# Sample units of an mLSTM decoder step: values, gates and keys turned in 32 by 32 squares by VectorE instead of by identity products on TensorE

## Chip, cores, metric

The kernel runs on one core of a Trainium2 chip. The metric is the device time of one execution in microseconds, and the time of a kernel is the median of several runs.

## What is computed

One inference step of a one-layer hybrid decoder: RMSNorm, one input projection (1024 to about 8200 columns), three parallel groups that read it, one output projection, residual and a final RMSNorm. A prompt of 2048 tokens and a sample group of 8 sequences with 8 tokens each go through the same layer. The change touches only the mLSTM group (4 heads of width 256) and of that only the sample group:

```
S    = (q k^T) * exp(Dm - m_t)                      # causal, per head
num  = w_inter * (q C) + S v
den  = w_inter * (q n) + sum(S)
h    = num / max(|den|, exp(-m_t))
C_new = w_C * C + sum_s w_s k_s v_s^T ;  n_new = w_C * n + sum_s w_s k_s
y_ml = rms_norm(sigmoid(o_pre) * h, g_head) * silu(z_ml)
```

C is a 256 by 256 matrix for each head and sequence, so the sample group has 32 of them, which are read and written.

## The kernel before

The program has three stages, one after the other on all engines: `project` (normalisation, all products with the input weights, which go to DRAM as channels by tokens), `attend` (cross-attention and convolution with their part of the output product) and `recur` (the mLSTM recurrence, its part of the output product, final norm). The change is in `recur`, the last 425 us or so.

`recur` goes over NT = 16 tiles t of 128 prompt tokens. TensorE does in each tile: `numerators(t)` (L2208, L2209), the eight state updates `update(t, j)` (L2223) with the output products of the tile before in between (`out_part(t - 1, g)`, L2256 to L2258), `scores(t + 1)` (L2184) and `turn_y(t)` (L2288, identity products that turn y). VectorE has for each tile: `add`, `first_half(t)`, `update(t, j)` with `turn_v`, `turn_keys` and `final_norm` between the updates, `second_half(t)` (L2660, L2665, which finishes y), `turn_o(t + 1)` (L2620), `score_weights(t + 1)` (L2558), `y_gate` and `y_low`. TensorE's `numerators(t + 1)` waits for `score_weights(t + 1)`.

The sample group is cut into UNITS = 8 units (4 sequences and one head each), with 32 tokens of a unit. Unit u is begun in tile t = 2u (`front_of`) and finished in tile 2u + 1 (`back_of`). Engines run their own instruction lists and meet by semaphores; the order in each list is the order of the code.

Values, output gates and keys of a unit lie in DRAM as channels by tokens, and the recurrence wants values, gates and one copy of the keys as tokens by channels, with token t of sequence j on partition 32j + t. Before the change `load_unit` on SyncE's queue fetches them as channels on 128 partitions in pieces of 8 tokens (32 bytes): four DMAs for values and gates (L1994) and two for keys (L1997). TensorE then turns them by products with the identity: four in `unit_turn_vo` (L2279) after `update(t, 6)` of an even tile, and two in `unit_front` (L2306) after `scores(t + 1)`. ScalarE takes values and gates out of PSUM in `unit_vo_back` (L2442, L2443) and the keys in its `unit_front` (L2471), scaled. The keys are also used as they are loaded, for the unit's scores (L2308), and that stays.

`load_unit` of unit u + 2 stands in SyncE's list at the end of iteration 2u + 2, behind the gates of the next tile; units 0 and 1 are loaded ahead of the loop. SyncE's list begins like this:

```python
sp.wait_ge(S["s_padded"], 3)
values(1)
load_unit(sp, 0, rest=False)
load_unit(sp, 0, states=False)
out_gates(1)
...
load_unit(sp, 1)
out_gates(2)
```

`values`, `out_gates` and `key_squares` already load the prompt tiles in squares of 32 by 32, which VectorE turns with its 32 by 32 block transposition (L2601, L2610, L2620). The prompt's keys, values and gates have been stored in that form since `project`.

## Time and profile before

| | us |
|---|---|
| median of 3 runs | 2056.63 |
| lowest and highest run | 2053.71, 2058.09 |
| the profiled execution, first to last instruction | 2055.3 |
| TensorE matmul busy in it | 2033.4 (99%) |
| VectorE busy | 1429.1 (70%) |
| ScalarE busy | 922.2 (45%) |
| GpSimd busy | 878.9 (43%) |

For the profiled execution the profile gives the span alone and no further time around it. Busy time on TensorE counts matmuls whose ends are modelled and overlap, so the distance from the start of one product to the start of the next says what a product costs, and not its duration. "L2279" is a line of the kernel before. SPq is SyncE's queue of DMA issues: the duration of its rows is the time of the issue, not of the transfer.

### The profile page before, as it was taken

How to read it: one execution, taken by the hardware profiler on the slowest of the kernel's cores; microseconds unless marked ns; L12 is line 12 of the kernel's file. 1: busy time of each engine (PE TensorE's matmuls, PEld its weight loads, DVE VectorE, ACT ScalarE, POOL GpSimd, SP SyncE). 2: the span in 40 equal slices, each digit the busy share in tenths (PEclk: the TensorE clock that was granted, in tenths of full speed). 3: DMA queues.
4: the chain of work that ended last, by engine and by line, in shares of the span. 5: the costliest groups of instructions: out<-in, count | busy, mean ns of one | idle time of the engine just before them, and what ended most of it. 6: DMA issues, size and time to landing. Idle time of an engine off the chain costs nothing.

```text
span 2055.3 us, 34212 instructions
## 1 busy us (share of the span) xinstructions
PE 2033.4 (99%) x12287; PEld 1892.5 (92%) x12287; DVE 1429.1 (70%) x2211; ACT 922.2 (45%) x1884; POOL 878.9 (43%) x720
## 2 busy tenths in 40 slices
PE   8999999999999999999999999999999999999998
PEld 5999999999999999999999999988888888888886
DVE  7667676688777666797777767644445477777774
ACT  5544445545445455454454455432224333343331
POOL 2465556575655555575555555510000122222320
PEclk9999999999999999999999999999999999999999
DMA  6634555555534555555345565677646788777754
GB/s 221 148 111 124 141 142 140 142 132 126 136 114 137 146 152 128 135 143 128 109 127 149 132 140 135 154 195 174 169 113 181 214 239 272 236 237 232 238 175 108
DMA packets 550983, 327.72 MB, mean 159 GB/s; under 512 B 283424, under 2 KB 514720, under 8 KB 550816
## 3 DMA queue, kind: packets, MB, share of 16 engines
q1 hardware_dynamic: 512672, 306.66, 55.1%
q10 hardware_dynamic: 36992, 14.68, 2.9%
q0 software_dynamic: 1152, 4.19, 0.6%
q8 instruction: 99, 1.62, 0.3%
q14 instruction: 68, 0.56, 0.1%
HBM read 232.16 MB, written 93.31 MB: 158 GB/s over the span
## 4 chain that ended last, share of the span: by engine, by line
PE 95%; DVE 2%; issue 1%; ACT 1%; ACTq 1%; DMA 0%; SPq 0%; DVEq 0%; POOLq 0%; POOL 0%
PE bank L707 21%; PE bank L709 21%; PE bank L708 21%; PE bank L2256 3%; PE bank L2258 3%; PE bank L2257 3%; PE bank L2223 3%; PE bank L2208 3%; PE bank L1653 1%; PE bank L1605 1%; PE bank L1655 1%; PE bank L1654 1%; PE bank L1640 1%; PE bank L1642 1%; PE bank L1641 1%; PE bank L2184 1%
## 5 line engine op out<-in xcount | busy, mean ns | idle before, releaser
L707 PE MATMUL bank<-xh,wh 128*128 128x352 f32 x2688 | 869.4, 323 | 2.1 <-DVE stage L1110 0.9
L709 PE MATMUL bank<-xh,wl 128*128 128x352 f32 x2688 | 865.9, 322 | 0.0
L708 PE MATMUL bank<-xl,wh 128*128 128x352 f32 x2688 | 862.9, 321 | 0.0
L1092 DVE TENSOR_TENSOR wl<-raw,wh 128x512 fp32r<-128x512 f32 x384 | 423.1, 1104 | 204.0 <-ACT wh L855 202.8
L707 PEld LDWEIGHTS bank<-xh,wh 128*128 128x128 f32 x2688 | 504.1, 188 | 5.5 <-issue 2.1
L709 PEld LDWEIGHTS bank<-xh,wl 128*128 128x128 f32 x2688 | 506.8, 189 | 0.0
L708 PEld LDWEIGHTS bank<-xl,wh 128*128 128x128 f32 x2688 | 506.0, 188 | 0.3 <-issue 0.2
L877 ACT ACTIVATE snap<-bank 128x352 f32<-128x352 f32 x384 | 178.7, 465 | 379.2 <-PE bank L709 379.2
L855 ACT ACTIVATE wh<-raw 128x512 fp32r<-128x512 f32 x384 | 240.7, 628 | 156.9 <-PE bank L709 155.2
L1092 DVE TENSOR_TENSOR wl<-wt,wh 128x512 fp32r<-128x512 f32 x288 | 237.9, 831 | 102.0 <-ACT wh L855 101.6
L655 POOL TENSOR_TENSOR stage<-snap 128x352 f32<-128x352 f32 x96 | 97.0, 1011 | 459.4 <-ACT snap L877 458.2
L855 ACT ACTIVATE wh<-wt 128x512 fp32r<-128x512 f32 x288 | 180.2, 626 | 118.0 <-PE bank L709 110.5
L639 POOL TENSOR_TENSOR wt<-raw 128x512 f32<-128x512 f32 x96 | 163.1, 1699 | 52.5 <-DMA raw<-in_w_in 51.1
L1110 DVE TENSOR_TENSOR stage<-bank,snap 128x352 f32<-128x352 f32 x288 | 149.2, 518 | 37.5 <-PE bank L709 31.5
L2110 POOL TENSOR_TENSOR work<-area,mask 128x512 f32<-128x512 f32 x16 | 20.4, 1278 | 337.2 <-DMA area<-scr_a 185.0
L643 POOL TENSOR_TENSOR raw<-raw 128x512 f32<-128x512 f32 x96 | 162.8, 1695 | 0.0
L642 POOL TENSOR_TENSOR wt<-raw,wt 128x512 f32<-128x512 f32 x96 | 154.6, 1610 | 7.5
L646 POOL TENSOR_TENSOR wt<-raw,wt 128x512 f32<-128x512 f32 x96 | 143.8, 1498 | 11.1 <-DVE wl L1092 11.1
L2256 PE MATMUL bank<-wm_h,out_yh 128*128 128x512 f32 x240 | 117.5, 490 | 0.0
L2258 PE MATMUL bank<-wm_h,out_yl 128*128 128x512 f32 x240 | 95.0, 396 | 0.0
L2653 DVE SCALAR_TENSOR_TENSOR m_wide<-m_wide,wcb,bank 128x257 f32<-128x257 f32 x120 | 57.0, 476 | 54.4 <-PE bank L2223 54.0
L2257 PE MATMUL bank<-wm_l,out_yh 128*128 128x512 f32 x240 | 94.8, 395 | 0.0
(343 smaller groups left out, 2603.3 us busy)
## 6 DMA issues: line engine op xcount, KB each, us to landing
raw<-in_w_in SPq DMA_DIRECT2D x72, 1024.0 KB, 5.7
raw<-in_w_in SPq DMA_DIRECT2D x48, 512.0 KB, 5.6
scr_vob<-stage SPq DMA_DIRECT2D x192, 88.0 KB, 3.5
scr_qk<-stage SPq DMA_DIRECT2D x48, 352.0 KB, 5.9
raw<-scr_qk SPq DMA_DIRECT2D x16, 1024.0 KB, 7.4
area<-scr_vob SPq DMA_DIRECT2D x32, 512.0 KB, 7.6
scr_z<-stage SPq DMA_DIRECT2D x24, 352.0 KB, 2.2
scr_xa<-stage SPq DMA_DIRECT2D x24, 352.0 KB, 2.5
```

The source lines that it names most:

```text
L639: pool.tensor_tensor(wt[:, 0], b12, b11, ALU.subtract).then_inc(S["t_ready"], 1)
L642: pool.tensor_tensor(wt[:, 1], b22, wt[:, 0], ALU.subtract).then_inc(S["t_ready"], 1)
L643: pool.tensor_tensor(b12, b22, b12, ALU.subtract).then_inc(S["t_ready"], 1)
L707: pe.matmul(out, wh[:, b, k, :], xh[:, b, k, :], start=(first and k == 0), stop=False, skip_group_check=True)
L708: pe.matmul(out, wh[:, b, k, :], xl[:, b, k, :], start=False, stop=False, skip_group_check=True)
L709: m = pe.matmul(out, wl[:, b, k, :], xh[:, b, k, :], start=False, stop=(k == 3), skip_group_check=True)
L855: act.activation(halves(q, b)[0], source(q, b), ACT.Copy).then_inc(S["w_high"], 1)
L877: act.activation(snap[:, n, :], g if n == 1 else b, ACT.Copy).then_inc(S["snap"], 1)
L1092: dve.tensor_tensor(low, source(q, b), high.bitcast(F32), ALU.subtract).then_inc(S["w_low"], 1)
L2256: pe.matmul(out, h[:, k, :], wmh[:, k, c], start=(k == 0), stop=False)
L2257: pe.matmul(out, h[:, k, :], wml[:, k, c], start=False, stop=False)
L2258: m = pe.matmul(out, l[:, k, :], wmh[:, k, c], start=False, stop=(k == KM - 1))
```

## The change

The six identity products of each unit go away. `load_unit` places values, gates and the second copy of the keys so that each 32 by 32 square holds 32 channels on 32 partitions by the 8 tokens of one sequence, and VectorE turns the squares. This takes 12 DMAs of 32 partitions each (three for each sequence j: values, gates, keys) where there were four of 128; the two loads of keys for the scores stay. A new function `unit_turn` on VectorE does three transpositions of 128 by 256 (gates, keys, values), ahead of `second_half(t)` in even tiles, and in tile 0 behind `score_weights(1)`. ScalarE applies Tanh to the gates in place and scales the keys in place.

```diff
@@ recur: sizes and places
-    UNIT_LOADS = 12
+    UNIT_LOADS = 20
+    svo = wide[:, 7632:8144]
+    skq = work[:, 1536:1792]
...
@@ load_unit
-        wait(dma, S["s_vo_turned"], u)
+        wait(dma, S["s_squares_turned"], 3 * u)
...
-        for a in range(4):
-            dma.dma_start(svo[a].rearrange("p (j x) -> p j x", j=4)[:, :, 0:DT],
-                         w["vo"][8 * (a // 2) + 2 * h + a % 2, :, cs].rearrange("p (j t) -> p j t", j=4)).then_inc(sem, 16)
+        for j in range(4):
+            rows, tokens = slice(SQ * j, SQ * (j + 1)), slice(SG * i + DT * j, SG * i + DT * (j + 1))
+            for n in range(2):
+                dma.dma_start(svo[rows, HD * n:HD * (n + 1)].rearrange("p (g x) -> p g x", x=SQ)[:, :, 0:DT],
+                              w["vo"][8 * n + 2 * h:8 * n + 2 * h + 2, :, tokens].rearrange("a (g r) t -> r (a g) t", r=SQ)).then_inc(sem, 16)
+            dma.dma_start(skq[rows, :].rearrange("p (g x) -> p g x", x=SQ)[:, :, 0:DT],
+                          w["qk"][8 + 2 * h:10 + 2 * h, :, T + SG * i + DT * j:T + SG * i + DT * (j + 1)].rearrange("a (g r) t -> r (a g) t", r=SQ)
+                          ).then_inc(sem, 16)
...
@@ TensorE
-        def unit_turn_vo(u):
-            pe.wait_ge(*unit_loads(u))
-            pe.wait_ge(S["t1_ready"], 4 * (2 * u) + 4)
-            pe.wait_ge(S["den_ready"], 2 * u + 1)
-            for a in range(4):
-                m = pe.transpose(bank[3][:, a * P:(a + 1) * P], svo[a], ident[:, :])
-            m.then_inc(S["s_vo_turned"], 1)
-
         def turn_y(t):
...
-            if front_of(t) is not None:
-                pe.wait_ge(S["s_vo_ready"], front_of(t) + 1)
...
-                pe.transpose(bank[SPARE][:, d * P:(d + 1) * P], skp[:, p, d, :], ident[:, :])
-            for d in range(2):
...
-            pe.wait_ge(S["s_v_ready"], u + 1)
+            pe.wait_ge(S["s_squares_turned"], 3 * u + 3)
+            pe.wait_ge(S["s_kw_ready"], u + 1)
...
-                    if j == 6 and front_of(t) is not None:
-                        unit_turn_vo(front_of(t))
...
@@ ScalarE
-        def unit_vo_back(u):
+        def unit_gates(u):
 
             p = u % 2
-            act.wait_ge(S["s_vo_turned"], u + 1)
-            if u == 0:
-                act.wait_ge(before["out_summed"], LAST_X)
-            wait(act, S["s_y_turned"], u - 1)
-            act.activation(sv[:, p, 0:HD], bank[3][:, 0:HD], ACT.Copy).then_inc(S["s_v_ready"], 1)
-            act.activation(so[:, p, :], bank[3][:, HD:2 * HD], ACT.Tanh, scale=0.5).then_inc(S["s_vo_ready"], 1)
+            act.wait_ge(S["s_squares_turned"], 3 * u + 1)
+            act.activation(so[:, p, :], so[:, p, :], ACT.Tanh, scale=0.5).then_inc(S["s_o_ready"], 1)
...
-            act.wait_ge(S["s_front"], u + 1)
-            act.activation(skw[:, :, :], bank[SPARE][:, 0:2 * P].rearrange("p (d x) -> p d x", d=2), ACT.Copy,
-                           scale=swsc[:, i, h:h + 1]).then_inc(S["s_kw_ready"], 1)
+            act.wait_ge(S["s_squares_turned"], 3 * u + 2)
+            act.activation(skw[:, :, :], skw[:, :, :], ACT.Copy, scale=swsc[:, i, h:h + 1]).then_inc(S["s_kw_ready"], 1)
...
-            if front_of(t) is not None:
-                unit_vo_back(front_of(t))
             keys(t + 1)
             if front_of(t) is not None:
+                unit_gates(front_of(t))
...
@@ VectorE
-        dve.memset(svo_wide, 0.0).then_inc(S["s_padded"], 1)
+        for tile in (svo, skq):
+            dve.memset(tile, 0.0).then_inc(S["s_padded"], 1)
...
+        def unit_turn(u):
+
+            p = u % 2
+            if u == 0:
+                dve.wait_ge(before["out_summed"], LAST_X)
+            dve.wait_ge(*unit_loads(u))
+            wait(dve, S["s_y_turned"], u - 1)
+            wait(dve, S["s_dC_summed"], u)
+            dve.transpose(so[:, p, :], svo[:, HD:2 * HD]).then_inc(S["s_squares_turned"], 1)
+            dve.transpose(skw.rearrange("p d x -> p (d x)"), skq).then_inc(S["s_squares_turned"], 1)
+            dve.transpose(sv[:, p, 0:HD], svo[:, 0:HD]).then_inc(S["s_squares_turned"], 1)
...
-            dve.wait_ge(S["s_kw_ready"], u + 1)
+            dve.wait_ge(S["s_front"], u + 1)
...
+                if j == 7 and t and front_of(t) is not None:
+                    unit_turn(front_of(t))
...
             if front_of(t) is not None:
+                if t == 0:
+                    unit_turn(0)
                 unit_weights(front_of(t))
```

VectorE's list at the end of tile 2 (unit 1), from the turned keys of tile 3 to the unit's score weights. Before (L2653 is `update`, L2660 and L2665 `second_half`, L2620 `turn_o`, L2558 `score_weights`, L2683 and L2687 `unit_weights`):

```order
L2610 STREAM_TRANSPOSE m_kw<-m_kb 128x1024
L2653 SCALAR_TENSOR_TENSOR m_wide<-m_wide,wcb,bank 128x257
L2660 SCALAR_TENSOR_TENSOR m_few<-m_few 128x4
L2665 TENSOR_SCALAR area<-area,m_few 128x256 x4
L2620 STREAM_TRANSPOSE m_wide<-area 128x1024
L2558 SCALAR_TENSOR_TENSOR work<-bank,work 128x512
L2683 COPY m_s_C<-nT 128x8
L2687 SCALAR_TENSOR_TENSOR m_wide<-bank,m_wide 128x32
```

After, where the same functions are L2640, L2647 and L2652, L2607, L2545, L2682 and L2686:

```order
L2597 STREAM_TRANSPOSE m_kw<-m_kb 128x1024
L2640 SCALAR_TENSOR_TENSOR m_wide<-m_wide,wcb,bank 128x257
L2676 STREAM_TRANSPOSE m_s_o<-m_wide 128x256
L2677 STREAM_TRANSPOSE work<-work 128x256
L2678 STREAM_TRANSPOSE m_s_v<-m_wide 128x256
L2647 SCALAR_TENSOR_TENSOR m_few<-m_few 128x4
L2652 TENSOR_SCALAR area<-area,m_few 128x256 x4
L2607 STREAM_TRANSPOSE m_wide<-area 128x1024
L2545 SCALAR_TENSOR_TENSOR work<-bank,work 128x512
L2682 COPY m_s_C<-nT 128x8
L2686 SCALAR_TENSOR_TENSOR m_wide<-bank,m_wide 128x32
```

Three transpositions (L2676 to L2678) stand between the last update and `second_half`; nothing else moved.

TensorE's list at the end of the same tile, from the last output products (L2257, L2258) over the scores (L2184) to the numerators of the next tile (L2208). Before:

```order
L2257 MATMUL bank<-wm_l,out_yh 128x512
L2258 MATMUL bank<-wm_h,out_yl 128x512
L2184 MATMUL bank<-raw 128x128 x8
L2306 MATMUL bank<-ident,m_s_kp 128x128 x2
L2308 MATMUL bank<-m_wide,m_s_kp 128x32 x2
L2288 MATMUL bank<-ident,area 128x128 x8
L2208 MATMUL bank<-m_wide 128x257 x2
```

After (L2263 and L2264, L2190, L2214):

```order
L2263 MATMUL bank<-wm_l,out_yh 128x512
L2264 MATMUL bank<-wm_h,out_yl 128x512
L2190 MATMUL bank<-raw 128x128 x8
L2302 MATMUL bank<-m_wide,m_s_kp 128x32 x2
L2284 MATMUL bank<-ident,area 128x128 x8
L2214 MATMUL bank<-m_wide 128x257 x2
```

The two products with the identity ahead of the unit's scores are gone. The four of L2279, which stood behind the seventh update of the tile, are gone in the same way.

SyncE's list for unit 0, from the unit's states to its output gate z. Before:

```order
L1990 DMA m_wide<-in_state_mlstm_C 128x4x256 x2
L1994 DMA m_wide<-scr_vo 128x4x8 x3
L1994 DMA m_s_vo<-scr_vo 128x4x8
L1997 DMA m_s_kp<-scr_qk 128x4x8 x2
L1999 DMA m_wide<-scr_qk 128x2x32
L2000 DMA m_wide<-scr_negr 128x32
L2001 DMA m_wide<-scr_a 128x32
L2002 DMA m_wide<-scr_z 128x2x32
```

After:

```order
L1991 DMA m_wide<-in_state_mlstm_C 128x4x256 x2
L1997 DMA m_wide<-scr_vo 32x8x8 x2
L1999 DMA work<-scr_qk 32x8x8
L1997 DMA m_wide<-scr_vo 32x8x8 x2
L1999 DMA work<-scr_qk 32x8x8
L1997 DMA m_wide<-scr_vo 32x8x8 x2
L1999 DMA work<-scr_qk 32x8x8
L1997 DMA m_wide<-scr_vo 32x8x8 x2
L1999 DMA work<-scr_qk 32x8x8
L2003 DMA m_s_kp<-scr_qk 128x4x8 x2
L2005 DMA m_wide<-scr_qk 128x2x32
L2006 DMA m_s_br<-scr_negr 128x32
```

Four DMAs of 128 partitions became twelve of 32, and everything behind them in the list stands eight DMAs later.

## Rows read from the trace of the kernel before

**Rows 1.** The profile's page: busy time by engine, and the chain by engine.

```profile
PE 2033.4 (99%) x12287; PEld 1892.5 (92%) x12287; DVE 1429.1 (70%) x2211; ACT 922.2 (45%) x1884; POOL 878.9 (43%) x720
PE 95%; DVE 2%; issue 1%; ACT 1%; ACTq 1%; DMA 0%; SPq 0%; DVEq 0%; POOLq 0%; POOL 0%
```

**Rows 2.** One line's instructions: durations in ns (min/median/max), first and last start.

```profile
L2306 PE MATMUL bank<-ident,m_s_kp x16: 272/273/273, 1651.9 to 1999.7; 128*128 128x128 f32 x16
```

**Rows 3.** Timeline of TensorE, updates of tile 6: start, us, instruction.

```profile
1793.61 0.60 PE L2223 MATMUL bank<-area,m_wide 128*128 128x257 f32 x2
...
1794.28 0.39 PE L2257 MATMUL bank<-wm_l,out_yh 128*128 128x512 f32 x1
...
1795.44 0.60 PE L2223 MATMUL bank<-area,m_wide 128*128 128x257 f32 x2
1795.88 0.49 PE L2279 MATMUL bank<-ident,m_wide 128*128 128x128 f32 x3
...
1796.55 0.39 PE L2257 MATMUL bank<-wm_l,out_yh 128*128 128x512 f32 x1
```

**Rows 4.** Timeline of TensorE, end of tile 6.

```profile
1799.55 1.95 PE L2184 MATMUL bank<-raw 128*128 128x128 f32 x16
1801.33 0.38 PE L2306 MATMUL bank<-ident,m_s_kp 128*128 128x128 f32 x2
1801.55 0.53 PE L2308 MATMUL bank<-m_wide,m_s_kp 128*128 128x32 f32 x4
...
1802.82 1.03 PE L2208 MATMUL bank<-m_wide 128*128 128x257 f32 x4
```

**Rows 5.** Timeline of VectorE, end of tile 6; in brackets idle time and its releaser.

```profile
1796.48 1.24 DVE L2610 STREAM_TRANSPOSE m_kw<-m_kb 128x1024 f32<-128x1024 f32 x1
1798.34 0.48 DVE L2653 SCALAR_TENSOR_TENSOR m_wide<-m_wide,wcb,bank 128x257 f32<-128x257 f32 x1 [0.63 <-PE bank L2223]
1798.74 0.15 DVE L2660 SCALAR_TENSOR_TENSOR m_few<-m_few 128x4 f32<-128x4 f32 x1
...
1799.99 1.24 DVE L2620 STREAM_TRANSPOSE m_wide<-area 128x1024 f32<-128x1024 f32 x1
1801.59 0.69 DVE L2558 SCALAR_TENSOR_TENSOR work<-bank,work 128x512 f32<-128x512 f32 x1 [0.37 <-issue]
...
1802.62 0.19 DVE L2687 SCALAR_TENSOR_TENSOR m_wide<-bank,m_wide 128x32 f32<-128x32 f32 x1 [0.26 <-ACT work L2471]
```

**Rows 6.** One line's instructions, as in rows 2: the transposition of 128 by 512.

```profile
L2601 DVE STREAM_TRANSPOSE area<-area x32: 655/705/714, 1634.5 to 1989.3; 128x512 f32<-128x512 f32 x32
```

**Rows 7.** Timeline of VectorE in an odd tile, tile 5.

```profile
1760.11 0.16 DVE L2693 COPY m_few<-bank 128x1 f32<-128x1 f32 x1 [0.25 <-PE bank L2324]
```

**Rows 8.** Timeline of SyncE's queue, loads of unit 0 and the next load.

```profile
1637.65 2.73 SPq L1994 DMA_DIRECT2D m_wide<-scr_vo  x3
...
1641.86 1.62 SPq L1997 DMA_DIRECT2D m_s_kp<-scr_qk  x2
...
1645.53 0.47 SPq L1405 DMA_DIRECT2D area<-scr_vob  x1
```

**Rows 9.** One line's issues, as in rows 2: `store_squares`, 32 partitions each.

```profile
L409 SPq DMA_DIRECT2D scr_vob<-stage x288: 303/541/7052, 63.4 to 1343.2; - x144
```

**Rows 10.** Timeline of all engines, tile 0 to the numerators of tile 1.

```profile
1634.17 0.38 DVE L2544 MEMSET m_wide<- 128x384 f32 x1 [3.53 <-PE bank L1642]
...
1649.87 1.06 ACT L2433 ACTIVATE area<-area 128x1024 f32<-128x1024 f32 x1 [4.80 <-DMA area<-scr_vob]
...
1652.23 0.66 DVE L2558 SCALAR_TENSOR_TENSOR work<-bank,work 128x512 f32<-128x512 f32 x1
...
1653.43 0.82 PE L2208 MATMUL bank<-m_wide 128*128 128x257 f32 x3
```

**Rows 11.** Timeline of VectorE, tile 2.

```profile
1688.73 0.71 DVE L2601 STREAM_TRANSPOSE area<-area 128x512 f32<-128x512 f32 x1 [0.48 <-DMA area<-scr_vob]
```

**Rows 12.** Waits of SyncE's queue, 1640 to 2000 us: total, times, longest.

```profile
SPq L1410 <- DVE out_yl L2589: 65.3, 12, 6.4
```

More of the change, by code:

```diff
@@ L1930, in recur @@
     sC = (wide[:, 5128:7184].rearrange("p (b d e) -> p b d e", b=4, d=2), overlay(0, "m_s_C", [P, 4, 2, HE]))
-    sq, sz, sbr = (wide[:, at:at + 128].rearrange("p (r d x) -> p r d x", r=2, d=2) for at in (7184, 7312, 7440))
-    snm, sW, ssw = (wide[:, at:at + SG] for at in (7568, 7600, 7632))
-    sqs = wide[:, 7664:7728].rearrange("p (d x) -> p d x", d=2)
-    swcb = wide[:, 7728:7760].rearrange("p (h b) -> p h b", h=H)
-    svo_wide, svo_last = wide[:, 7760:8144], overlay(35072, "m_s_vo", [P, P])
-    svo = [*(svo_wide[:, a * P:(a + 1) * P] for a in range(3)), svo_last[:, :]]
+    sq, sz, sbr = (a.rearrange("p (r d x) -> p r d x", r=2, d=2)
+                   for a in (wide[:, 7184:7312], wide[:, 7312:7440], overlay(35072, "m_s_br", [P, P])[:, :]))
+    snm, sW, ssw = (wide[:, at:at + SG] for at in (7440, 7472, 7504))
+    sqs = wide[:, 7536:7600].rearrange("p (d x) -> p d x", d=2)
+    swcb = wide[:, 7600:7632].rearrange("p (h b) -> p h b", h=H)
+    svo = wide[:, 7632:8144]
+    skq = work[:, 1536:1792]
     nm, sw = (work[:, i * H * P:(i + 1) * H * P].rearrange("p (h t) -> p h t", h=H) for i in range(2))
@@ L2528, in _ @@
         ch = Chain(dve, S["m_step"])
-        for tile in (skp.ap(), svo_last[:, :]):
-            dve.memset(tile, 0.0).then_inc(S["s_padded"], 1)
+        dve.memset(skp.ap(), 0.0).then_inc(S["s_padded"], 1)
         dve.wait_ge(before["xa_split"], TILES)
```

3 lines of the change are left out of this document (2 added, 1 removed).

## Prediction

> **What bounds the kernel now.** I read the page first: TensorE is busy for 99% of the span and holds 95% of the chain that ended last; VectorE holds 2% [rows 1]. So a removed product on TensorE is worth its time, if nothing it waits for becomes later. Then the lines of the removed work, then the timelines of the engines around the two places where it stands. The durations are no prices here: one identity product is listed with 272 ns [rows 2], while two of them start within 0.22 us of what follows (1801.33 to 1801.55) [rows 4], because they overlap. VectorE, with 70%, has room on average; what counts is whether it has room just before TensorE waits for it. That is so at the end of an even tile: score_weights(t + 1) ends at 1801.59 + 0.69 = 1802.28 [rows 5], and the numerators that wait for it begin at 1802.82 [rows 4]. The room is 0.54 us, less some 0.1 us for the hand-over (the scores end at 1799.55 + 1.95 = 1801.50 and VectorE starts on them at 1801.59 [rows 4, 5]).
>
> **What TensorE no longer does.** From the start of the update product to the second output product behind it takes 1.11 us with the four identity products between (1795.44 to 1796.55) and 0.67 us without (1793.61 to 1794.28) [rows 3]: they cost 0.44 us. The two of the keys cost 0.22 us [rows 4]. Together 0.66 us for each unit, 5.3 us for eight. ScalarE's removed copy of the values lies beside this work and earns nothing.
>
> The Trainium skill ("TensorE: Matmul & The Clock Gate", Part 4: PE-mode transpose) gives a transpose in the context of one kernel as about 275 ns. The duration agrees with the row's 272 ns, but taken as a price it would make 48 x 0.275 = 13.2 us of the removed work. The distance between starts decides, and gives 5.3.
>
> **What VectorE does more.** The trace has transpositions of 512 and 1024 columns: 0.705 us [rows 6] and 1.24 us [rows 5], so 0.54 us for 512 columns more, and 0.44 us for 256. The next instruction starts 0.08 us before the one ahead of it is listed as ended (1798.34 + 0.48 against 1798.74 [rows 5]), so each takes 0.36 us of VectorE's list, three take 1.07. Bounds: 0.27 each if they went by columns alone, 0.44 if nothing overlaps, so 0.8 to 1.3 for three.
>
> In an even tile from tile 2 on, in the times of rows 5: the last update waits for TensorE (0.63 idle) and comes with TensorE's saving, at 1798.34 - 0.44 = 1797.90; the turned keys, done at 1796.48 + 1.24 = 1797.72, don't hold it back. The transpositions start 0.40 later, at 1798.30, and second_half at 1799.37 instead of 1798.74, 0.63 later. turn_o goes from 1799.99 to 1800.62. score_weights had 0.37 of idle time in front of it, which is used up: it starts at 1800.62 + 1.24 - 0.08 = 1801.78 and ends at 1802.47. TensorE could begin the numerators at 1802.82 - 0.66 = 1802.16, and gets the weights at about 1802.57. So it stalls for 0.41 us that it did not before, and of 0.66 there remain 0.25. With the bounds of the transpositions (0.8 to 1.3) it is 0.52 to 0.02. y itself comes in time: its products start behind the unit's scores, and y is ready at 1799.99 + 0.08 + 0.63 = 1800.7, ahead of them in any case (1801.55 + 0.37 - 0.66 = 1801.3 [rows 4]).
>
> Behind that, VectorE lies 0.4 us nearer to TensorE than before. In front of the unit's score weights it waited 0.26 us for the scaled keys [rows 5]; these now come from VectorE's own squares and are early. In the odd tile it has another 0.25 us of waiting for the unit's numerator [rows 7]. 0.5 against 0.4: no further stall. Units 1 to 7 thus give 7 x 0.25 = 1.8 us.
>
> **What SyncE's queue does more.** The four loads of unit 0 take from 1637.65 to 1641.86, 4.2 us or 1.05 each, while the states of 1 MB drain ahead of them [rows 8]. The new ones have the same bytes for values and gates, and half of that again for the keys: 3072 pieces of 32 bytes instead of 2048. The nearest row for a DMA of 32 partitions is store_squares, 704 pieces each, with a median issue of 0.54 us [rows 9]. I take it that the first eight, which hold the old pieces, are issued in the time of the old four, since 8 x 0.54 = 4.3, and the four for the keys come on top: 4 x 0.54 = 2.1 us for a unit. Lower bound: +1.5 us (14 DMAs at 0.53 = 7.4 against the 5.8 that the six took, 1637.65 to 1643.48 [rows 8]). Upper bound: each of the eight more costs 1.05, +8.4 us.
>
> For units 2 to 7 this is hidden. SyncE waits up to 6.4 us in each two tiles for y's low part [rows 12], and the loads are asked for a tile later.
>
> For unit 0 it is not. The output gates of tile 1 are issued behind it, at 1645.53 [rows 8], and ScalarE waits 4.80 us for them, until 1649.87; turn_o and score_weights(1) (1652.23, end 1652.89) follow without a gap, and the numerators of tile 1 start at 1653.43 [rows 10]. With the wait of 0.1 for the hand-over they had 0.44 to spare. Two things delay the gates: 2.1 us of issues, and the clearing of 768 instead of 384 columns (0.38 us [rows 10]) in front of the first turned values, some 0.3. Less 0.1 of gap in front of turn_o: 2.1 + 0.3 - 0.1 - 0.44 = 1.9 us later. unit_turn(0) stands behind score_weights(1), in front of the gating of y for tile 0: 1.07 us of VectorE in a stretch where it then waits for TensorE anyway. The saving of unit 0 itself (0.66) is inside this wait and can't be counted.
>
> Load 1 now waits until unit 0's squares are turned, which is some 0.5 us after SyncE gets there, and is itself 2.1 longer. All that is issued behind it comes 0.3 + 2.1 + 0.5 + 2.1 = 5 us later, against a TensorE that is 1.9 later: net 3.1. The values of tile 3 already arrived 0.48 us late for VectorE [rows 11]. VectorE then stalls 3 us in tile 2, where it has waits like the 0.63 us in front of the update in rows 5 to catch up; I put 0.5 us of that on TensorE, bounds 0 and 3.1.
>
> **Sum.** -1.8 + 1.9 + 0.5 = +0.6 us on the profiled span of 2055.3. That execution lies 1.3 us under the median of the runs shown, so in terms of the median 2056.6 + 0.6 = 2057.2. Less than 4.1 us (0.2%) to either side can't be told from no change.
>
> **Rivals.**
> - *All of TensorE's work comes back.* For it: 99% busy. If VectorE's three transpositions found cover in full and the start hid the loads: -5.3, 2051.3. Against it: 0.54 us of room for 0.63 us of delay and 0.66 of earlier arrival. If only the stall is absent and the start is as above: -4.6 + 2.4 = -2.2, 2054.4, no change.
> - *Slower: the start pays for each DMA.* If each of the eight more costs 1.05 us, as rows 8 have it, the gates of tile 1 come 8.4 us later: 8.4 + 0.3 - 0.1 - 0.44 = +8.2 at the numerators of tile 1, and with the units' 1.8 the kernel ends at +6.4 or more, 2063. It decides from about 0.7 us for each added DMA on (5.6 + 0.3 - 0.54 + 0.5 - 1.8 = 4.1). For it: the measured 1.05. Against: these were issued behind 1 MB of states, and rows 9. The Trainium skill ("DMA: Bandwidth & Descriptors", Rules for kernel authors) speaks against this part of the change: many small transfers should be one large one, and under 64 KB one pays mostly overhead; these go from 16 KB to 8 KB. Here that would matter only by SyncE's issue time in front of tile 1.
> - *VectorE is late in the odd tile too.* If the 0.4 us were not caught up by the 0.5 of waits, for instance because transpositions take 0.44 each, TensorE would lose another 0.3 for each unit: +2 to +3, 2059.5.
> - *No effect anywhere*, by chance of cancelling terms, is what I forecast; it is not that the change does nothing: TensorE's busy time must fall.
>
> **How the numbers follow.** Forecast with hand-over stall and late start, 2055 to 2060: 0.50. All of it back: 0.12. Stall absent, start late: 0.14. Price for each DMA at the start: 0.15. Late in the odd tile: 0.09. Faster by over 0.2% is the second case, 0.12. Slower is the fourth, a part of the fifth and the forecast's upper end: 0.15 + 0.05 = 0.20. The rest, 0.68, is within. The range leaves out the ends of the second and the fourth case: 2052.3 to 2062.0.
>
> **What would show it.** Right: the row of score_weights in even tiles without idle time in front, a start of the numerators set by it, and a pair of tiles shorter by 0.2 to 0.3 us than before; the numerators of tile 1 some 2 us later; issues of 0.5 us for the DMAs of 32 partitions. Wrong: a pair shorter by 0.66 (then VectorE's list has more room than I count), issues near 1 us, or a stall in the updates of odd tiles. It would be wrong most likely by the start, where one late load delays all engines.

## The result, and the profile of the changed kernel

The changed kernel takes 2060.61 us (median of 16 runs, 2056.45 to 2065.54), the kernel before 2057.14 (16 runs, 2052.34 to 2059.23). The ratio is 1.0021, with a 95% interval of 1.0013 to 1.0029: slower by 4.3 us, 2.7 to 6.0 (the two medians themselves differ by 3.5). The time is inside the range given, 3.4 us above the forecast time and 0.6 above the band of 2055 to 2060 that had half of the chances. The difference lies at the 4.1 us (0.2%) below which the prediction speaks of no change, and its interval reaches to both sides of them.

The page of the changed kernel has this of busy time, of the chain that ended last, and of transfers:

```profile
PE 2037.5 (99%) x12239; PEld 1895.0 (92%) x12239; DVE 1434.6 (70%) x2235; ACT 919.3 (45%) x1876; POOL 878.5 (43%) x720
...
PE 93%; SPq 2%; DVE 1%; issue 1%; DMA 1%; ACT 1%; ACTq 1%; POOL 0%; DVEq 0%; POOLq 0%
```

48 TensorE products are gone, and TensorE is busy for longer (2037.5 us against 2033.4 in [rows 1]); its share of the chain is lower by two points. The rise lies in the stages ahead of the one that was changed: up to the first scores of `recur` the view by windows has 1626.93 us of busy time against 1620.97, and behind them 410.61 against 412.38, so in the changed stage the busy time fell by 1.8 us (1.7 in the second pair of profiles). The span is 2061.5 us against 2055.3. Of these 6.2 us, 3.9 lie ahead of the third stage, where nothing was changed: TensorE's first scores of `recur` start at 1638.65 here and at 1634.73 before. Over the fourteen profiles of this study this start lies between 1630.98 and 1638.65 without regard to the version (two profiles of the kernel before: 1632.94, 1634.73; the two lowest, 1630.98 and 1631.44, are of changed kernels). So I compare the third stage alone, from those scores to the end of the span, and below "+20.56" is a time from the first scores on.

| from the first scores, us | before | before, again | after | after, again |
|---|---|---|---|---|
| numerators of tile 1 | 18.70 | 18.45 | 20.56 | 20.28 |
| scores(2) | 42.45 | 41.84 | 45.45 | 45.14 |
| scores(4) | 92.02 | 91.41 | 96.10 | 96.20 |
| a pair of tiles, mean of five from tile 4 on | 49.58 | 49.57 | 49.28 | 49.28 |
| end of the span | 420.57 | 419.96 | 422.85 | 422.99 |

The third stage is 2.3 to 3.0 us longer. All of the loss, and more, is there by scores(4); from there on each pair gives back 0.3 us. Of the 422.85 us TensorE is idle for 12.2, of the 420.57 before for 8.2: the waits grew by 4.1 us while its work shrank by 1.8.

**The steady part.** First TensorE's timeline at the end of tile 6, which answers to [rows 4] (L2190 scores, L2302 the unit's scores, L2284 y's products, L2214 numerators):

```profile
1806.81 1.95 PE L2190 MATMUL bank<-raw 128*128 128x128 f32 x16
1808.59 0.53 PE L2302 MATMUL bank<-m_wide,m_s_kp 128*128 128x32 f32 x4
1808.96 1.07 PE L2284 MATMUL bank<-ident,area 128*128 128x128 f32 x8
1810.15 1.11 PE L2214 MATMUL bank<-m_wide 128*128 128x257 f32 x4
```

and VectorE's in the same stretch, which answers to [rows 5]:

```profile
1805.62 0.48 DVE L2640 SCALAR_TENSOR_TENSOR m_wide<-m_wide,wcb,bank 128x257 f32<-128x257 f32 x1 [0.20 <-PE bank L2229]
1806.02 0.43 DVE L2676 STREAM_TRANSPOSE m_s_o<-m_wide 128x256 f32<-128x256 f32 x1
1806.38 0.40 DVE L2677 STREAM_TRANSPOSE work<-work 128x256 f32<-128x256 f32 x1
1806.70 0.40 DVE L2678 STREAM_TRANSPOSE m_s_v<-m_wide 128x256 f32<-128x256 f32 x1
1807.03 0.12 DVE L2647 SCALAR_TENSOR_TENSOR m_few<-m_few 128x4 f32<-128x4 f32 x1
...
1808.24 1.24 DVE L2607 STREAM_TRANSPOSE m_wide<-area 128x1024 f32<-128x1024 f32 x1
1809.40 0.65 DVE L2545 SCALAR_TENSOR_TENSOR work<-bank,work 128x512 f32<-128x512 f32 x1
...
1810.04 0.18 DVE L2686 SCALAR_TENSOR_TENSOR m_wide<-bank,m_wide 128x32 f32<-128x32 f32 x1
```

The three transpositions take from 1806.02 to 1807.03. score_weights(7) (L2545) has no idle time ahead of it, ends at 1810.05, and the numerators start 0.10 later. From the scores to the numerators TensorE needs 3.34 us, against 3.27 before, though 0.22 us of products between them is gone. So 0.29 us of stall is new there, and it shows as a distance only: no bracket stands at 1810.15. Another 0.07 us stands directly behind it: the first four products of the numerators are listed with 1.11 us here and with 1.03 before [rows 4].

**The start.** SyncE's queue with the loads of unit 0, which answers to [rows 8] (duration of the issues; L1997 values and gates, L1999 the turned copy of the keys, L2003 the keys for the scores, L1405 gates of tile 1):

```profile
1641.74 0.99 SPq L1997 DMA_DIRECT2D m_wide<-scr_vo  x2
1642.77 0.45 SPq L1999 DMA_DIRECT2D work<-scr_qk  x1
...
1644.74 1.83 SPq L1997 DMA_DIRECT2D m_wide<-scr_vo  x2
...
1648.76 1.00 SPq L2003 DMA_DIRECT2D m_s_kp<-scr_qk  x2
...
1651.82 0.47 SPq L1405 DMA_DIRECT2D area<-scr_vob  x1
```

Twelve issues take 7.02 us, 0.59 each, where four took 4.21, so 2.8 us more. They begin 0.2 us later after the first scores, the issues behind them are 0.6 shorter than before, and the gates of tile 1 are issued at +13.17 instead of +10.80, 2.4 us later. The timelines of ScalarE, VectorE and TensorE behind that, which answer to [rows 10]:

```profile
1656.20 1.06 ACT L2426 ACTIVATE area<-area 128x1024 f32<-128x1024 f32 x1 [7.21 <-DMA area<-scr_vob]
1657.29 1.25 DVE L2607 STREAM_TRANSPOSE m_wide<-area 128x1024 f32<-128x1024 f32 x1 [3.79 <-ACT area L2426]
1658.46 0.65 DVE L2545 SCALAR_TENSOR_TENSOR work<-bank,work 128x512 f32<-128x512 f32 x1
...
1659.21 1.81 PE L2214 MATMUL bank<-m_wide 128*128 128x257 f32 x4 [3.05 <-DVE work L2545]
1660.82 1.06 PE L2215 MATMUL bank<-area,work 128*128 128x257 f32 x2
1661.67 1.64 PE L2214 MATMUL bank<-m_wide 128*128 128x257 f32 x4
1663.14 0.60 PE L2215 MATMUL bank<-area,work 128*128 128x257 f32 x2
1663.58 1.03 PE L2214 MATMUL bank<-m_wide 128*128 128x257 f32 x4
```

Each step is as in the prediction: the gates late, then ScalarE, turn_o, score_weights(1), and the numerators at +20.56 instead of +18.70. Then something that it does not have. The same group of four is listed with 1.81 us at 1659.21 and 1.03 at 1663.58. Two heads, twelve products, take 4.37 us (1659.21 to 1663.58); before they took 2.61 (1653.43 to 1656.04). The table by windows has the granted clock in its third column from the right (start:end, length, busy us of five engines, clock, DMA share, GB/s):

```profile
1659.20:1661.20 2.00, 1.99 (x5) 1.63 (x6) 1.94 (x7) 1.12 (x4) 0.00 (x0) 0.57 0.82 185
1661.20:1662.80 1.60, 1.60 (x5) 1.28 (x4) 1.44 (x3) 1.08 (x2) 0.00 (x0) 0.50 0.53 155
...
1663.60:1666.00 2.40, 2.40 (x13) 2.06 (x11) 0.97 (x4) 0.00 (x0) 0.01 (x1) 1.00 0.81 306
```

and this is the same pair of heads in the kernel before:

```profile
1653.40:1656.00 2.60, 2.60 (x14) 2.29 (x13) 2.31 (x5) 1.28 (x3) 0.00 (x0) 1.00 0.80 199
```

Behind 3.05 us of idle time TensorE ran at 0.50, 1.2 of 2.4 GHz, and was back at full clock by 1663.6. The late gates cost 1.86 us as a wait and 1.76 as a slow clock. The Trainium skill ("TensorE: Matmul & The Clock Gate", Part 1) has these two levels, the lower one for an array that has been idle. These rows agree.

**The second unit.** VectorE's timeline in tile 2, which answers to [rows 11], with its waits (L2569 gating of y, L2588 values of tile 3, L2561 final norm):

```profile
1688.00 1.29 DVE L2569 TENSOR_TENSOR area<-bank,area 128x512 f32<-128x512 f32 x2 [0.96 <-DMA area<-scr_z]
...
1697.54 0.71 DVE L2588 STREAM_TRANSPOSE area<-area 128x512 f32<-128x512 f32 x1 [2.37 <-DMA area<-scr_vob]
...
1704.33 1.28 DVE L2561 SCALAR_TENSOR_TENSOR m_acc<-m_acc,m_few,m_gf 128x1024 f32<-128x1024 f32 x1 [1.84 <-POOL m_few L2142]
```

The transposition of the values, 0.48 us late before, is 2.37 late now, and TensorE waits at the end of the tile:

```profile
1707.58 2.05 PE L2190 MATMUL bank<-raw 128*128 128x128 f32 x16 [0.55 <-DVE m_wide L2640]
...
1711.59 1.11 PE L2214 MATMUL bank<-m_wide 128*128 128x257 f32 x4 [0.68 <-issue]
```

From scores(2) to scores(4) it takes 50.65 us (96.10 - 45.45), against 49.57 before. With the 0.30 that a pair saves otherwise, tiles 2 and 3 cost 1.4 us (1.8 in the other profile of this kernel). Not all of it is the second unit's longer load: e3 below has the loads of before, and its tiles 2 and 3 take 49.78 us, 0.5 more than its later pairs. Its VectorE also waits longer for the values of tile 3 than in the kernel before (1.49 us), and has the three transpositions behind that. So 0.9 to 1.3 us are the added loads'.

### The profile page after: what moved, and what is told of

The parts are those of the page before. It is cut to its first block, busy times and chain, and to the rows that moved or that the text cites. A ratio compares the mean times of both kernels' runs of the same rounds, so it can differ in the third digit from the quotient of the medians.

```text
span 2061.5 us, 34204 instructions
## 1 busy us (share of the span) xinstructions
PE 2037.5 (99%) x12239; PEld 1895.0 (92%) x12239; DVE 1434.6 (70%) x2235; ACT 919.3 (45%) x1876; POOL 878.5 (43%) x720
## 4 chain that ended last, share of the span: by engine, by line
PE 93%; SPq 2%; DVE 1%; issue 1%; DMA 1%; ACT 1%; ACTq 1%; POOL 0%; DVEq 0%; POOLq 0%
PE bank L707 21%; PE bank L709 21%; PE bank L708 21%; PE bank L2262 3%; PE bank L2264 3%; PE bank L2263 3%; PE bank L2214 2%; PE bank L2229 2%; PE bank L1653 1%; PE bank L1605 1%; PE bank L1640 1%; PE bank L1655 1%; PE bank L1654 1%; PE bank L1642 1%; PE bank L1641 1%; PE bank L775 1%
## 5 line engine op out<-in xcount | busy, mean ns | idle before, releaser
L2264 PE MATMUL bank<-wm_h,out_yl 128*128 128x512 f32 x240 | 95.0, 396 | 0.0
L2263 PE MATMUL bank<-wm_l,out_yh 128*128 128x512 f32 x240 | 94.8, 395 | 0.0
L2640 DVE SCALAR_TENSOR_TENSOR m_wide<-m_wide,wcb,bank 128x257 f32<-128x257 f32 x120 | 56.8, 475 | 46.0 <-PE bank L2229 45.1
```

Of the source, the lines that this page charges most:

```text
L2263: pe.matmul(out, h[:, k, :], wml[:, k, c], start=False, stop=False)
L2264: m = pe.matmul(out, l[:, k, :], wmh[:, k, c], start=False, stop=(k == KM - 1))
```

## The experiments

All are timed against the kernel before on the same chip. The third stage is read from one profile of each; two profiles of one kernel differ in it by 0.1 to 0.6 us.

| run | median us | ratio to before (95%) | numerators(1) | scores(2) | scores(4) | pair | third stage |
|---|---|---|---|---|---|---|---|
| e1_again | 2060.86 | 1.0023 (1.0014, 1.0032) | 20.28 | 45.14 | 96.20 | 49.28 | 422.99 |
| e2_new_loads_only | 2063.68 | 1.0034 (1.0022, 1.0046) | 22.56 | 45.67 | 96.57 | 49.57 | 425.12 |
| e3_old_loads_only | 2056.40 | 0.9999 (0.9990, 1.0008) | 18.59 | 41.97 | 91.75 | 49.27 | 418.46 |
| e4_gates_first | 2059.66 | 1.0020 (1.0011, 1.0030) | 17.73 | 40.82 | 97.90 | 49.28 | 424.68 |
| e5_before_again | 2057.64 | 1.0001 (0.9992, 1.0010) | 18.45 | 41.84 | 91.41 | 49.57 | 419.96 |
| e6_turn_late | 2059.40 | 1.0013 (1.0004, 1.0022) | 20.68 | 45.74 | 95.57 | 49.38 | 422.46 |
| e7_gates_prologue | 2057.63 | 1.0001 (0.9991, 1.0012) | 17.39 | 40.52 | 93.55 | 49.27 | 420.27 |
| e8_before_gates_prologue | 2057.39 | 1.0000 (0.9991, 1.0008) | 18.77 | 42.13 | 91.70 | 49.57 | 420.20 |
| e9_turn_twice | 2068.01 | 1.0052 (1.0037, 1.0066) | 20.49 | 46.19 | 97.13 | 50.41 | 430.67 |
| e10_spread | 2056.83 | 0.9994 (0.9984, 1.0003) | 20.70 | 45.57 | 96.76 | 48.91 | 421.32 |
| e11_spread_order | 2058.08 | 1.0003 (0.9991, 1.0014) | 17.50 | 41.20 | 98.06 | 48.91 | 422.60 |
| e12_before_order | 2056.90 | 0.9994 (0.9984, 1.0004) | 18.54 | 41.73 | 91.29 | 49.57 | 419.84 |

### e1_again and e5_before_again: both kernels once more

> The changed kernel once more, for a second profile: it tells what of the difference lies in the third stage and what in the stages ahead of it, which the change does not touch. Theory A (the start of the recurrence pays about 4 us, units 2 to 7 give 0.3 us a pair of tiles back): from the first scores of the third stage to the end 422.9 us within 0.5, against 420.6 before; the distance from scores to scores over two tiles 49.29 us again; the rest of the span varies by 2 to 4 us from one execution to the next. Rival B (the stages ahead have become slower through the change, by way of where instructions or buffers lie): their length is 4 us above the one before here too.

> The kernel before once more, for a second profile of it. So far its one profile has the third stage at 420.6 us and the first scores at 1634.7, against 1635.1 to 1638.6 in five profiles of changed kernels. Theory A (the stages ahead differ from execution to execution alone): the third stage is 420.6 us within 0.5, and the first scores lie between 1635 and 1638. Rival B (the change makes the stages ahead some 2 us longer, which would explain that the medians differ by 4 to 5 us and the third stages by 2.3): the first scores lie at 1634.7 or earlier again.

The changed kernel comes out at 1.0023, the kernel before at 1.0001 of itself. The second profile of the changed kernel has the same idle time at the same place (3.06 us), the same slow twelve products (1655.39 to 1659.76, 4.37 us) and the same pair of 49.28. The loss in the third stage is the kernel's and not that of one execution. The first scores are another matter: those of e5 (1632.94) are not between 1635 and 1638, as theory A had them, but earlier than 1634.7, as rival B had them. Rival B still fails, on later runs: the changed kernels of e6 and e10 have theirs at 1631.44 and 1630.98. What these starts go with is told under "What stays open".

### e2_new_loads_only: the kernel before with the twelve small loads

The loads and their places in memory are those of the changed kernel; the identity products stay, and turn what was loaded. The sample units' values are in another order by that, so the output is not the reference's.

```diff
-        for a in range(4):
-            dma.dma_start(svo[a]..., w["vo"][8 * (a // 2) + 2 * h + a % 2, :, cs]...)
+        for j in range(4):
+            for n in range(2):
+                dma.dma_start(svo[rows, ...], w["vo"][8 * n + 2 * h:..., :, tokens]...)
+            dma.dma_start(skq[rows, :]..., w["qk"]...)
```

> The kernel before with the loads and the clearing of the changed one, and the identity products kept. The values, gates and keys then lie in the wrong order, so the sample outputs are not the reference's. Theory A (loads cost at the start alone): the numerators of tile 1 come 2 us or more after their place in the kernel before, with the clock penalty if TensorE idles some 3 us; the whole third stage is 4 to 5 us longer, 425 us, and the pair of tiles keeps its 49.58 us. Rival C (the loads cost in each unit too, by SyncE's queue or by contention): the pair becomes longer than 49.7.

The third stage is 425.12 us, as theory A has it. The pair is 49.57, as before: from unit 2 on the twelve loads are hidden. The start costs more than in the changed kernel, and in front of other work. In TensorE's timeline it is the unit's first identity product that waits for the loads:

```profile
1652.03 1.11 PE L2285 MATMUL bank<-ident,m_wide 128*128 128x128 f32 x4 [3.47 <-DMA m_wide<-scr_z]
```

All of TensorE's list stands behind these products; the changed kernel has none there, and its waits come later.

### e3_old_loads_only: the changed kernel with the six loads of before

VectorE turns what lies in the old places; the second copy of the keys stays zero, so the sample's output is not the reference's. This takes the small loads away and keeps everything else.

```diff
-        for j in range(4):
-            ... (twelve DMAs of 32 partitions)
+        for a in range(4):
+            dma.dma_start(svo[:, a * P:(a + 1) * P]..., w["vo"][..., :, cs]...)
```

> The changed kernel with the six loads that a unit had before (values and gates in four DMAs of 128 partitions, no second copy of the keys, whose buffer stays zero): the sample outputs are not the reference's. Theory A: the start costs nothing, numerators of tile 1 within 0.4 us of their old place, the pair of tiles 49.29 us as with the change, so the third stage takes 420.6 - 7.5 x 0.29 = 418.4 us and the kernel is about 2 us faster than before. Rival C (loads cost in each unit): the pair becomes shorter than 49.2.

The numerators of tile 1 are back at +18.59, scores(4) at +91.75, the pair stays at 49.27, and the third stage takes 418.46 us, 1.5 to 2.1 less than before. So with its start as it was, the change would have given what the prediction counts for the units, and the whole net loss of the third stage is the loads'. The time, 0.9999, is not faster than before; 1.5 to 2.1 us lies at the edge of what it can tell (0.9990 is 2.1 us). The timeline of TensorE at the numerators of tile 1:

```profile
1654.13 1.11 PE L2209 MATMUL bank<-m_wide 128*128 128x257 f32 x4 [1.56 <-DVE work L2540]
```

and the window of two heads behind it:

```profile
1654.10:1656.70 2.60, 2.57 (x12) 2.29 (x13) 2.38 (x8) 1.70 (x5) 0.00 (x0) 1.00 0.80 194
```

TensorE was idle for 1.56 us ahead of them, and its clock stayed at 1.00.

### e9_turn_twice: the suspected cost doubled

The three transpositions are done twice, the second time behind a wait for the first.

```diff
+            dve.transpose(so[:, p, :], ...).then_inc(S["extra"], 1)   (and keys, values)
+            dve.wait_ge(S["extra"], 3 * u + 3)
             dve.transpose(so[:, p, :], ...).then_inc(S["s_squares_turned"], 1)
```

> The changed kernel with the three transpositions of units 0 to 7 done twice, the second time behind a wait for the first. Theory A (VectorE's list in front of the score weights sets when TensorE goes on, so that each further microsecond there is one of the kernel): the pair of tiles grows by 1.07 us and a hand-over of 0.1, from 49.28 to 50.4 to 50.5, and the third stage by 8 to 9 us, to 431. Rival G (the 0.3 us that is left of the saving has another reason, such as a product that became slower): the pair grows by less than 0.5.

In VectorE's timeline the second set starts 1.13 us behind the first (1805.13, 1806.26), and a pair becomes 1.13 longer, 50.41. What stands on VectorE ahead of score_weights at this place is paid in full by TensorE; the change's own 0.36 (0.29 of stall and 0.07 behind it) is the part that had no room. The start of this kernel shows something else: its numerators of tile 1 also wait 2.99 us, and behind that the two heads take 5.21 us (1656.12 to 1661.33) and not 4.37:

```profile
1656.10:1661.30 5.20, 5.18 (x12) 4.18 (x13) 4.95 (x14) 2.19 (x5) 0.00 (x0) 0.50 0.76 227
```

The same idle time cost 2.6 us of slow clock here and 1.76 in the changed kernel.

### e6_turn_late: the transpositions behind the score weights

```diff
-                if j == 7 and t and front_of(t) is not None:
-                    unit_turn(front_of(t))
...
             if front_of(t) is not None:
-                if t == 0:
-                    unit_turn(0)
+                unit_turn(front_of(t))
                 unit_weights(front_of(t))
```

> The changed kernel with the three transpositions of every unit behind the score weights, as in tile 0, instead of in front of the second half. Theory A (in even tiles TensorE waits for VectorE's score weights by what the transpositions add in front): this stall of 0.4 us goes and the pair of tiles falls from 49.28 to 48.9 us, the full 0.66 below the kernel before; third stage 420.7, as the start stays late. Rival E (VectorE is then late in the odd tile, where it had 0.5 us of waits for 1.07 us of transpositions): TensorE waits in the first updates of the odd tile and the pair stays at 49.2 or above.

The pair is 49.38, no better than 49.28, so that full return did not come. TensorE's timeline shows where the wait went, into the updates of the odd tile:

```profile
1808.94 0.70 PE L2229 MATMUL bank<-area,m_kw 128*128 128x257 f32 x2
1810.55 0.67 PE L2229 MATMUL bank<-area,m_kw 128*128 128x257 f32 x2 [0.22 <-DVE m_s_o L2694]
```

1.61 us between two updates that are 1.24 apart in e10 below. VectorE's list has room between score weights and that place for less than 1.07 us.

### e10_spread: the transpositions between the updates

```diff
-    def unit_turn(u):
+    def unit_turn(u, which=(0, 1, 2)):
...
-                if j == 7 and t and front_of(t) is not None:
-                    unit_turn(front_of(t))
+                if j in (2, 4) and t and front_of(t) is not None:
+                    unit_turn(front_of(t), (0,) if j == 2 else (1, 2))
```

> The changed kernel with the transpositions of units 1 to 7 put between the updates of the even tile, where VectorE waits 1.35 us for TensorE: the gates behind the third update, keys and values behind the fifth. Theory A: neither the numerators of the odd tile nor its first updates are held, the pair of tiles falls to 48.92 us, all 0.66 below the kernel before; third stage 422.9 - 7 x 0.36 = 420.4, as the start stays late. Rival H (the full 0.66 is not to be had, because the products without the identity products pay for it elsewhere): the pair stays above 49.1.

In this kernel the pair is 48.91, 0.66 less than before: all of the removed TensorE work returns, when the transpositions stand where VectorE waits for TensorE anyway. TensorE's timeline has no stall at either place; it goes from the scores to the numerators in 3.06 us, and the odd tile's updates are 1.24 apart:

```profile
1799.42 1.95 PE L2190 MATMUL bank<-raw 128*128 128x128 f32 x16
...
1802.48 1.03 PE L2214 MATMUL bank<-m_wide 128*128 128x257 f32 x4
...
1809.20 0.70 PE L2229 MATMUL bank<-area,m_kw 128*128 128x257 f32 x2
1810.44 0.60 PE L2229 MATMUL bank<-area,m_kw 128*128 128x257 f32 x2
```

The third stage is 421.32, 0.9 more than the 420.4 expected. The start is as late as in the changed kernel, and tile 2 takes 24.94 us against 23.48. VectorE's timeline has the waits of the changed kernel there, each longer:

```profile
1681.72 1.29 DVE L2569 TENSOR_TENSOR area<-bank,area 128x512 f32<-128x512 f32 x2 [2.24 <-DMA area<-scr_z]
...
1691.45 0.71 DVE L2588 STREAM_TRANSPOSE area<-area 128x512 f32<-128x512 f32 x1 [2.97 <-DMA area<-scr_vob]
...
1698.23 1.28 DVE L2561 SCALAR_TENSOR_TENSOR m_acc<-m_acc,m_few,m_gf 128x1024 f32<-128x1024 f32 x1 [2.59 <-POOL m_few L2142]
```

z of tile 1 was issued at +45.50, against +44.27 in the changed kernel. Whether the transpositions have a part in that, one profile doesn't tell; no transposition of unit 1 has a wait of its own. The kernel takes 2056.83 us. Against the changed kernel that is some 4 us less, by medians taken at different times; from the kernel before it is not told apart (0.9984 to 1.0003).

### e4_gates_first, e7_gates_prologue, e8_before_gates_prologue: SyncE's order

e4 issues the gates of tile 1 within the load of unit 0:

```diff
-        load_unit(sp, 0, states=False)
-        out_gates(1)
+        load_unit(sp, 0, states=False, between=lambda: out_gates(1))   (behind the first of the four sequences)
```

> The changed kernel with the output gates of tile 1 loaded after three of the twelve square loads of unit 0, instead of behind all of unit 0. Theory A: the numerators of tile 1 are released by unit 0's loads then and no more by the gates; they come 2.5 to 3 us earlier than in the changed kernel, TensorE idles less than 1 us in front of them and keeps its full clock (1.8 us more); the cost of the second unit's load in tiles 2 and 3 (1.4 us) stays. Third stage 419 us. Rival D (something else in tile 1 holds them, for instance the turned squares on VectorE): under 1 us is gained.

The first half of the expectation held: numerators of tile 1 at +17.73, scores(2) 4.6 us earlier than in the changed kernel. The second did not: tile 2 took 29.92 us instead of 23.48 and ate it. The view of waits of this kernel, from the stage's start into tile 3 (total us, times, longest), has:

```profile
ACT area L2427 <- DMA area<-scr_vob: 11.1, 2, 10.0
DVE area L2589 <- DMA area<-scr_vob: 5.0, 2, 4.4
DVE area L2608 <- ACT area L2427: 4.6, 1, 4.6
DVE area L2570 <- DMA area<-scr_z: 4.2, 1, 4.2
```

The gates of tile 2, z of tile 1 and the values of tile 3 stand behind unit 1's loads in SyncE's list. In the changed kernel z and the values were late by 0.96 and 2.37 us, with a TensorE that came to tile 2 4.6 us later. e7 moves the store of the last sums and the gates of tile 2 ahead of unit 1's loads as well, and e8 makes the moves of e7 in the kernel before:

```diff
-        load_unit(sp, 1)
-        out_gates(2)
-        sp.dma_start(gf[:, :], ...)
         sp.wait_ge(before["res_added"], LAST_X)
         sp.dma_start(w["acc"][T:TT, :], ...)
+        out_gates(2)
+        load_unit(sp, 1)
+        sp.dma_start(gf[:, :], ...)
```

> As the run with the gates of tile 1 first, and SyncE's list ahead of the loop in another order too: the store of the last sums and the output gates of tile 2 ahead of unit 1's load, so that the 5 us wait for that store's landing lies beside the load. Theory A (in that run TensorE won 4.6 us in tile 1 and lost 6.4 in tile 2, because z of tile 1 and the gates and values of tiles 2 and 3 came late behind unit 1's load and the store): scores(2) at +40.8 as there, the waits of 4.2 and 4.6 us in tile 2 shrink to under 1, scores(4) at +91 instead of +97.9; third stage 418 us. Rival F (the DMA engines themselves are the limit in this stretch, not SyncE's order): scores(4) stays above +95.

> The same two moves in SyncE's list on the kernel before. Theory A: it lacks the eight more DMAs, so it had less to lose: the wait of 4.80 us for the gates of tile 1 goes, and the third stage becomes 1 us shorter or stays, 419.5 to 420.6, the pair of tiles stays at 49.58. Then the changed kernel with these moves is 1.5 to 2 us faster than this one.

e7 reaches scores(4) at +93.55, between what an order problem alone and a transfer problem alone would give, and a third stage of 420.27: with another order the changed kernel is level with the one before (2057.63 against 2057.39 for e8). In the kernel before the same moves change nothing (420.20). That the changed kernel would then be 1.5 to 2 us faster than this one did not come true.

### e11_spread_order and e12_before_order: both remedies together

e11 has the edits of e10 and e4, and loads unit 1 in the loop, behind the gates of tile 3. e12 has these moves of loads in the kernel before.

```diff
-        load_unit(sp, 1)
         out_gates(2)
...
                 out_gates(t + 2)
+                if t == 1:
+                    load_unit(sp, 1)
```

> The kernel with the spread transpositions, the gates of tile 1 ahead of most of unit 0's loads, and unit 1's load moved from ahead of the loop to tile 1 in SyncE's list, behind the loads for tile 3. Theory A (the start is late because the loads of tiles 1 to 3 stand behind the loads of units 0 and 1): numerators of tile 1 at +17.4, scores(2) at +40.5, no wait over 1 us in tile 2, scores(4) at +89.5 against +96.1; third stage 422.9 - 6.3 - 2.5 = 414, 6 us faster than the kernel before. Rival F (the transfers themselves are the limit there): unit 1 comes late now, and scores(4) stays above +92.

> The same order of SyncE's list on the kernel before, with its identity products and its six loads for each unit. Theory A: without the longer loads the start has little to lose; scores(4) between +91 and +92 as before, the pair at 49.57, third stage 419.5 to 420.5. What the run before this one gains over it is then the worth of the change once its costs are hidden: 7.5 x 0.66 and the wait for unit 0, some 5 to 6 us.

The pair is 48.91 again and scores(2) comes at +41.20, but scores(4) at +98.06, and the third stage is 422.60 instead of some 414. The timelines of VectorE and TensorE name the reason:

```profile
1699.24 0.45 DVE L2680 STREAM_TRANSPOSE m_s_o<-m_wide 128x256 f32<-128x256 f32 x1 [9.04 <-DMA m_wide<-scr_z]
...
1700.11 1.23 PE L2231 MATMUL bank<-area,m_wide 128*128 128x257 f32 x2 [5.38 <-DVE m_wide L2642]
```

With the transposition of the gates after update 2, VectorE needs unit 1 early in tile 2, and loaded this late it comes 9 us too late. My two remedies exclude each other in this form. A version that takes unit 1's transpositions at the end of tile 2, those of the later units between the updates, and e7's order was not tried. From e7's third stage and the 0.36 that each later pair gains in e10 it would be some 2 us shorter than e7, near 418; this is an estimate.

## Why the prediction was right, and where it was not

**What TensorE no longer does: right for the distances, wrong for the page.** 0.66 us for each unit. e10, which removes the same products and hides the transpositions, has a pair shorter by exactly 0.66 (49.57 to 48.91). The distance between starts was the price, not the listed 272 ns. "TensorE's busy time must fall" did not hold for the page (+4.1 us), because the stages ahead were busy for 6.0 us more; in the third stage it fell, by 1.8.

**What VectorE does more: right, with a slightly smaller stall.** Three transpositions took 1.01 us (forecast 1.07), score_weights started 2.59 us behind the scores (forecast 2.67), without idle time ahead of it, and the new stall is 0.29 at the numerators. A pair gained 0.30 us (forecast 0.25). e9 shows that VectorE's list at this place is paid by TensorE, and e10 that the other 0.36 returns when the transpositions leave it.

**Late in the odd tile: not in the changed kernel, but near.** The changed kernel's pair has 0.07 us more than the stall (0.66 less 0.29 of stall is 0.37, and 0.30 was gained). It isn't in the odd tile's updates: beside e10, whose numerators are not held, the whole of it lies between the first and the second product of the numerators, 0.29 us apart here and 0.22 there. e6 shows that 1.07 us behind the score weights do bring this stall.

**The start: wait right, price not.** The gates' delay of 2.4 us (forecast 2.1 + 0.3) and the numerators' 1.86 us (forecast 1.9) are as worked out, the first of them with some luck: the issues took 2.8 more and not 2.1, the later beginning was 0.2 and not 0.3, and the 0.6 by which the issues behind became shorter is not in the prediction. Issues of 32 partitions took 0.59 us, and eight more of them 2.8 us in all, so the rival with 1.05 for each is out. The Trainium skill's rule against many small transfers ("DMA: Bandwidth & Descriptors", Rules for kernel authors) points the right way here. It does so only because the issues stand in front of tile 1; from unit 2 on they cost nothing (e2). The step that failed is that the sum has the 1.9 at the numerators and nothing else for the start: the wait makes the idle time of TensorE 3 us long, and behind it two heads ran at the lower clock for +1.76. The stretch to scores(2) gave 0.6 back in one pair of profiles and 0.3 in the other, so the start cost 3.0 and 3.3 instead of 1.9. The idle time is longer than the delay because 1.56 us of it are there with the old loads too (e3): TensorE's own wait for unit 0's loads (0.94 us in the kernel before, at the first identity product of unit 0) and the identity products have gone from in front of it.

**The second unit: mis-sized.** I put 0.5 us on TensorE, with bounds 0 and 3.1; tiles 2 and 3 cost 1.4 and 1.8, of which 0.5 is not the added loads' (e3).

**The sum.** With what was measured, in the first pair of profiles: +3.00 to scores(2), +1.08 to scores(4), five pairs at -0.30 to scores(14), -0.41 for tile 14, whose saving is counted ahead of its stall, and +0.11 behind: +2.3 us in the third stage. In the second pair it is +3.0. Forecast was +0.6. What was left out is a clock term of 1.8; the term for tiles 2 and 3 was too small by 0.9 to 1.3; 0.3 to 0.6 was given back. Both errors go the same way. That the time is still inside the range is in part luck: its upper end was set with the price for each DMA in view, which is not what happened.

**What stays open.** The timed difference is 2.7 to 6.0 us, the third stages differ by 2.3 and 3.0. The rest, up to some 3 us, could lie in the stages ahead, whose end varies by 7.7 us over the profiles. That variation goes with the granted clock at two places that the change doesn't touch, near the start of the program and near 1390 us. The mean granted clock of the windows 5:25 and 1380:1400, for all fourteen profiles:

| clock in 5:25 | clock in 1380:1400 | first scores of `recur`, us |
|---|---|---|
| 1.00 | 0.91 | 1630.98 (e10), 1631.44 (e6) |
| 0.91 | 0.91 | 1632.94 (e5) |
| 0.91 | 0.83 | 1634.36 (e12) |
| 0.83 | 0.91 | 1635.11 (e1), 1635.40 (e8), 1635.54 (e3), 1636.22 (e4) |
| 0.83 | 0.83 | 1634.73 (before) |
| 0.91 | 0.74 | 1635.63 (e9), 1635.88 (e2) |
| 0.83 | 0.74 | 1636.10 (e11), 1636.53 (e7), 1638.65 (after) |

The rows of the second window of the changed kernel and of e10 are

```profile
1380.00:1400.00 20.00, 14.80 (x58) 12.04 (x57) 7.02 (x14) 4.39 (x13) 0.72 (x1) 0.74 0.70 137
1380.00:1400.00 20.00, 16.42 (x78) 13.99 (x79) 10.67 (x24) 7.92 (x24) 0.72 (x1) 0.91 0.68 157
```

In all fourteen profiles TensorE has an idle time of 3.5 to 4.3 us there, and the clock around it is low for longer in some than in others, as between e9 and the changed kernel above. Both ends of the table have changed kernels. Whether the timed runs of the changed kernel meet the lower clock ahead of `recur` more often than those of the kernel before is not shown: they list one mean clock for the whole execution.

## What to carry to other kernels

Where one work list is moved from TensorE to another engine, look for the place on that engine where it waits for TensorE anyway: the same three transpositions were worth 0.30 us a pair at the end of the tile and 0.66 between the updates. A queue that is idle in the steady state is not idle at the start of a stage: price added issues at the first consumer behind them, and when that one is mended expect the next load in the list to bind. And a wait on TensorE that becomes long enough to lower its clock costs more than it lasts: behind 3 us of idle time it was 1.8 us more here, and 2.6 in e9. In a sum of stalls, ask how long the idle time becomes as a whole, not by how much it grows.

## What the hardware showed that I had not expected

A single idle time of TensorE changes the clock of the work behind it. In the third stage of these runs, idle time ahead of a product, and the granted clock behind it:

| kernel | idle, us | granted clock behind it |
|---|---|---|
| e3 | 1.56 | 1.00 over 2.6 us |
| e4, tile 2 | 2.20 | 0.68 over 4.0 us |
| e6 | 2.96 | 0.61 over 4.3 us |
| e9 | 2.99 | 0.50 over 5.2 us |
| e10 | 3.00 | 0.61 over 4.4 us |
| after | 3.05 | 0.61 over 4.4 us |
| e1 | 3.06 | 0.61 over 4.4 us |
| e2 | 3.47 | 0.50 over 2.8 us |
| e11, tile 2 | 5.38 | 0.50 over 4.9 us |

The length of the idle time alone does not give the price: e9 and the changed kernel differ by 0.06 us in it and by 0.8 us in what follows. In e4 another 1.30 us of idle time ends 5 us ahead of the 2.20. Its window, with the clock third from the right:

```profile
1686.40:1690.40 4.00, 3.98 (x13) 3.26 (x14) 3.84 (x11) 1.17 (x2) 0.00 (x0) 0.68 0.99 244
```

and that of e10:

```profile
1651.60:1656.00 4.40, 4.32 (x12) 3.54 (x13) 4.11 (x11) 2.19 (x5) 0.00 (x0) 0.61 0.86 216
```

The second thing was the order of loads. The kernel before doesn't care about it (e8, e12: third stages of 420.20 and 419.84 against 419.96 and 420.57), while with eight small DMAs more for each unit the moves of e8 bring the numerators of tile 1 forward by 3 us and make tile 2 longer by 2.4 (e7 against the changed kernel).
